# Two blocks of a transformer on one core: another order of the first loads and products, and the gather for the first experts

## The chip, the cores and the metric

The kernel runs on one core of a Trainium2 chip. The metric is the device time of one execution in microseconds (us); three runs of the kernel before gave 2827.01 to 2830.11 us, median 2827.8.

## The reference, cut to what matters

Everything is float32, 256 tokens of width 1024. A first block of two layers (attention of two kinds and an MLP) is followed by a second block (a token mixer and a mixture of 16 experts).

```python
cos, sin = rope_tables(positions)
cond = jax.nn.silu(c)
for l in range(2):
    mod = (cond @ ada_w[l] + ada_b[l])                      # 1024 -> 6 * 1024
    shift_m, scale_m, gate_m, shift_f, scale_f, gate_f = jnp.split(mod, 6, axis=-1)
    h = rms_norm(x, norm_mix_g[l]) * (1.0 + scale_m) + shift_m
    proj = h @ w_in[l]                                      # queries, keys: norm, then rope
    ...
# second block, at its end:
gates, idx = lax.top_k(jnp.swapaxes(affinity, 1, 2), 32)    # each of 16 experts picks 32 of 256 tokens
xe = h[idx]
hid = silu(xe @ exp_w1) * (xe @ exp_w3)                     # 1024 -> 2048
ye = hid @ exp_w2 * gates                                   # 2048 -> 1024, added back at idx
```

## The kernel before, in words

**Loads.** SyncE walks through a list of weight chunks of 2 MB (`weight_chunks`) and loads each into a slot of SBUF as soon as the chunk that held the slot was used. For the first block there are four slots (the ring), for the experts six, and three more that are used once for the chunks of expert 0. What "used" means is a count of TensorE's jobs: SyncE waits on `bank_full` for the last job of the earlier chunk. The engines' orders are written out by hand; every engine works strictly in its own order. The class `Jobs` holds the order of all PSUM jobs; job n goes to bank n mod 8 and waits until job n - 8 was emptied by VectorE ("v") or ScalarE ("s").

**Head.** SyncE issues the vectors (0.22 MB: biases, gains, c) and then the ring: four chunks of ada_w for layer 0 in the order `ADA_ORDER = [2, 3, 0, 1]` (2 and 3 give scale, 0 and 1 give shift), then w_in. GpSimd issues, on its own queue, positions, lambdas, the early constants (identity, means), x, and, once the fourth chunk of ada_w has landed (L2167), the late constants. TensorE waits for vectors and `cond`, then per chunk makes a raw product (L2694, `four_sums`: 8 products of 512 columns in four strips), which ScalarE copies out, and later turns the sum into columns with four small products (L2686); VectorE adds the bias. Before the third chunk TensorE waits for constants and x and transposes x (L2698, 16 transposes, four banks, copied to `xT` by VectorE, L2494). Before the fourth it takes the mean of squares of x (L2717), for which ScalarE squares `xT` (L2205). VectorE starts with the angles of rope and the lambdas (L2465 to L2487), ScalarE with the sines (L2249 to L2253) right after the silu. At the end VectorE scales `xT` into `hT` (`scaled`, L2395), ScalarE adds the shift slice by slice (`shifted`, L2222), and TensorE starts on the columns of queries and keys (L2686), two `columns` of 256 tokens per job, whose squares ScalarE takes (L2285). GpSimd rotates them (L2181) with `rope`.

**Experts.** The one-hot matrix `E_SEL` (tokens by 16 x 32 places) picks each expert's tokens. For expert 0 a product with its 32 columns gives `xc` (jobs "xc"); the gather for all 16 experts (jobs "xe", eight times two products of 512 columns) runs inside expert 0, four j after the second quarter of its first layer and four after the third. From then on VectorE copies the next expert's columns of it to `E_XC`. An expert uses 12 chunks: w1 and w3 by quarters (L2694), small turnings (L2686), then w2 by quarters and `combine`. Expert 0 is written out, experts 1 to 14 are a loop, expert 15 is written out.

Of the kernel before, what the change touches and what calls it, by code (L numbers as in the profile page):

```python
# [9 lines left out]
ALU = mybir.AluOpType  # L10
# [408 lines left out]
class Jobs:  # L419


    def __init__(self):
# [3 lines left out]
        for n, c in enumerate(ADA_ORDER):  # L426
            if n == 2:
                for tt in range(TT):
                    for q in range(2):
                        add(("xT", tt, q), "v")  # L430
            if n == 3:
                add(("norm", "mix", 0), "s")
            self.modulations([("ada", 0, c)])
# [105 lines left out]
    def second_block(self):  # L539
# [74 lines left out]
        for e in range(N_EXP):  # L614
            for q in range(4):
# [24 lines left out]
GATHERED_AFTER = [(), (0, 1, 2, 3), (4, 5, 6, 7), ()]  # L640
# [14 lines left out]

EXPERT_JOBS = 24
# [20 lines left out]
E_XE, E_EARLY, E_XTOK, E_GAIN, E_H2, E_ACC = 0, 4096, 4096, 6144, 9472, 9472  # L677
E_U, E_SQ, E_DIAG = 7424, 0, 2048
# [3 lines left out]
def build(nc, t, out):  # L682
# [24 lines left out]
    with ExitStack() as ctx:  # L707
# [297 lines left out]
        def second_pool(pool, chain):  # L1005
# [55 lines left out]
            pool.wait_ge(xc_ready, N_EXP - 1)  # L1061
# [3 lines left out]
        def second_scalar(act, chain, free, norm, shifted):  # L1065
# [149 lines left out]
            def expert(k0, more, done):  # L1215
                for q in range(4):
# [43 lines left out]
            expert(0, 0, free)  # L1260
            with act.Fori(1, N_EXP - 1) as e:
                expert(1, e - 1, free.looped)
            free.skip(N_EXP - 2)
# [8 lines left out]
        def second_vector(dve, chain, free, norm):  # L1272
# [332 lines left out]
            for tt in range(TT):  # L1605
                last = one_hot(tt, 0, 1)
            last.then_inc(chosen, 1)
            for tt in range(TT):
                last = one_hot(tt, 1, N_EXP)
# [3 lines left out]
            def expert(k0, e, more, done):  # L1613
# [12 lines left out]
                if k0 == 0:  # L1626
                    emptied(dve, ("xe", KT - 1))
                if k0 < N_EXP - 1:
# [28 lines left out]
            expert(0, 0, 0, free)  # L1657
            with dve.Fori(1, N_EXP - 1) as e:
                expert(1, e, e - 1, free.looped)
            free.skip(N_EXP - 2)  # L1660
# [14 lines left out]
        def second_tensor(pe, start, finish, chunk, product, four_sums, turn, columns, norm, normed, done):  # L1675
# [44 lines left out]

            def keep_busy(b, n):

                for _ in range(n):
                    nc.tensor.matmul(b[:, :], ident, cst[:, 0:512], start=True, stop=True)  # L1724
# [305 lines left out]
            emptied(pe, ("slotT", 0))  # L2030

            def expert(k0, e, more):
# [31 lines left out]
                xc, hid = ar(E_XC, KT, CAP), ar(E_HID, 16, CAP)  # L2064
                if k0 == 0:
                    emptied(pe, ("xc", 0, 1))
                else:
                    pe.wait_ge(xc_ready, e)
                for q in range(4):
# [19 lines left out]
                    if k0 == 0:  # L2089
# [18 lines left out]
            expert(0, 0, 0)  # L2108
            with pe.Fori(1, N_EXP - 1) as e:
                expert(1, e, e - 1)  # L2110
            done[0] += EXPERT_JOBS * (N_EXP - 2)
# [6 lines left out]
        def _(sp):  # L2118
            def middle_experts():
                first = chunk_at[("w1", 2, 0)]  # L2120
                with sp.Fori(2, N_EXP - 1) as e:
                    for i in range(12):
                        n = first + i
                        key, name = chunks[n][0], chunks[n][1]
                        sp.wait_ge(bank_full, jobs.last_job_of_chunk[chunks[n - EXPERT_SLOTS][0]] + 1 + (e - 2) * EXPERT_JOBS)
# [4 lines left out]
            sp.dma_start(vec[:, :], t["vectors"]).then_inc(vectors_loaded, 16)  # L2130
            for n, (key, *_rest) in enumerate(chunks):
                if key[0] in ("w1", "w2", "w3") and 2 <= key[1] < N_EXP - 1:
                    if key == ("w1", 2, 0):
# [62 lines left out]
        def _(act):  # L2196
# [51 lines left out]
            act.wait_ge(angles_ready, 1)  # L2248
            nc.scalar.activation(rope[:, 1, :], ar(0, SEQ), ACT.Sin, scale=col("rot_sign")).then_inc(rope_ready, 1)  # L2249
            act.wait_ge(angles_ready, 2)  # L2250
            nc.scalar.activation(rope[:, 0, :], ar(256, SEQ), ACT.Sin).then_inc(rope_ready, 1)
            act.wait_ge(lam_sums, 1)
            nc.scalar.activation(lamv[:, 0:2 * DEPTH], lamv[:, 4:4 + 2 * DEPTH], ACT.Exp).then_inc(lam_exp, 1)  # L2253
            for n, c in enumerate(ADA_ORDER):
                if n == 3:
                    emptied(act, ("xT", 1, 1))
                    norm("mix", 0, xT, None, None)
                modulations([("ada", 0, c)])
            modulations([])

            for l in range(DEPTH):
# [106 lines left out]
        def _(dve):  # L2368
# [95 lines left out]
            dve.wait_ge(small_loaded, 32)  # L2464
# [608 lines left out]
```

## Time and profile before

| | us |
|---|---|
| three runs, median | 2827.8 |
| profiled execution | 2835.8 |
| its span | 2833.9 |
| TensorE busy | 2527.0 (89%) |
| VectorE busy | 894.4 (32%) |
| ScalarE busy | 532.3 (19%) |
| granted TensorE clock, mean | 0.925 |

The span runs from the first to the last instruction that the profile shows. TensorE's matmuls are pipelined, so its busy time holds waits inside a matmul as well. Each product of float32 stands as two records. The granted clock is 1.00 or 0.50 of 2.4 GHz; a value between them is a mixture in the window. 666.85 MB are moved; an expert chunk is 2048 KB, 192 of them are the experts'.

### The profile page before, as it was taken

To read this page: it belongs to the slowest core of one execution; us is meant where nothing else is said; L and a number is where in the kernel's file an instruction comes from. 1 tells how busy PE (TensorE), PEld (TensorE's weight loads), DVE (VectorE), ACT (ScalarE), POOL (GpSimd) and SP (SyncE) were. 2 spreads that over 40 slices of the span, in tenths; PEclk is the share of its full clock that TensorE was granted. 3 is DMA by queue.
4 is the path that set the end of the run, shared out by engine and by line. 5 is a ranking of instruction groups with operands and counts; after the bars stand their busy time and mean duration, and the time that the engine had idled before them with its cause. 6 is when DMAs were issued, how large, how long until landed. Compare 5 with 4: busy or idle time off the path is not lost.

```text
span 2833.9 us, 36842 instructions
## 1 busy us (share of the span) xinstructions
PE 2527.0 (89%) x15512; PEld 1792.9 (63%) x15512; DVE 894.4 (32%) x1609; ACT 532.3 (19%) x1063; POOL 154.2 (5%) x146
## 2 busy tenths in 40 slices
PE   5999989999999899999989999999877777777777
PEld 4857678887867788887568888864433333333333
DVE  2743524202735412313575641231111111111112
ACT  2115411001126212002234432121000000000001
POOL 0320000000310000000011110100000000000000
PEclk8999999999999999999999999989788887878888
DMA  7335447545332463453000002548999999999998
GB/s 298 137 139 231 195 184 278 221 150 210 146 134 75 149 256 132 182 234 115 1 1 1 1 2 97 214 196 366 428 428 429 428 428 429 429 428 428 429 429 356
DMA packets 48787, 666.85 MB, mean 235 GB/s; under 512 B 5531, under 2 KB 5702, under 8 KB 7585
## 3 DMA queue, kind: packets, MB, share of 16 engines
q1 hardware_dynamic: 46656, 656.65, 57.0%
q0 software_dynamic: 2016, 8.53, 0.9%
q8 instruction: 90, 1.47, 0.2%
q14 instruction: 25, 0.20, 0.0%
HBM read 664.11 MB, written 1.05 MB: 235 GB/s over the span
## 4 chain that ended last, share of the span: by engine, by line
PE 64%; DMA 26%; DVE 6%; ACT 2%; issue 1%; POOL 0%; DVEq 0%; ACTq 0%; POOLq 0%
PE bank L2686 51%; DMA ring<-exp_w 24%; PE bank L2694 6%; PE bank L2698 2%; PE bank L2910 2%; DVE arena L2420 1%; PE bank L1886 1%; DMA arena<-x 1%; DMA arena<-exp_w 1%; PE bank L2717 1%; PE bank L1914 1%; PE bank L1724 1%; ACT hT L2222 0%; DVE hT L2563 0%; ACT arena L2346 0%
## 5 line engine op out<-in xcount | busy, mean ns | idle before, releaser
L2686 PE MATMUL bank<-hT,ring 128*128 128x256 f32 (+2 forms) x3232 | 740.3, 389 | 11.3 <-ACT hT L2222 11.3
L2686 PEld LDWEIGHTS bank<-hT,ring 128*128 128x128 f32 x3232 | 607.7, 192 | 146.3 <-issue 70.9
L2694 PE MATMUL bank<-ring,arena 128*32 128x512 f32 (+1 forms) x2496 | 322.8, 659 | 170.2 <-DMA ring<-exp_w 157.2
L2686 PE MATMUL bank<-arena,ring 128*128 128x256 f32 x1600 | 352.1, 381 | 6.7 <-POOL arena L2189 2.8
L2686 PEld LDWEIGHTS bank<-arena,ring 128*128 128x128 f32 x1600 | 304.2, 191 | 50.0 <-POOL arena L2189 3.6
L2694 PEld LDWEIGHTS bank<-ring,arena 128*32 128x32 f32 x2496 | 88.2, 130 | 357.0 <-issue 209.7
L2686 PEld LDWEIGHTS bank<-vec,arena 128*128 128x128 f32 x1344 | 177.6, 213 | 74.6 <-issue 67.6
L2686 PE MATMUL bank<-arena 64*128 64x128 f32 (+4 forms) x1156 | 207.7, 378 | 4.7 <-ACT arena L2329 1.6
L2694 PE MATMUL bank<-arena 128*32 128x256 f32 (+1 forms) x1568 | 162.4, 557 | 39.8 <-DMA arena<-exp_w 39.4
L1623 DVE COPY arena<-bank 128x512 f32<-128x512 f32 x64 | 44.3, 692 | 481.7 <-PE bank L2694 481.7
L2686 PE MATMUL bank<-vec,arena 128*128 128x32 f32 (+2 forms) x1344 | 183.1, 289 | 3.9 <-DVE arena L2420 3.4
L2686 PEld LDWEIGHTS bank<-arena 64*128 64x128 f32 (+1 forms) x1156 | 139.1, 196 | 66.3 <-issue 48.7
L2694 PEld LDWEIGHTS bank<-arena 128*32 128x32 f32 x1568 | 57.2, 128 | 128.8 <-issue 64.6
L2529 DVE RECIPROCAL arena<-arena 128x512 f32<-128x512 f32 x28 | 93.9, 3353 | 84.3 <-ACT arena L2274 84.3
L2686 PE MATMUL bank<-ring 128*128 128x128 f32 (+1 forms) x1024 | 110.2, 268 | 5.1 <-DVE ring L1442 4.9
L2686 PEld LDWEIGHTS bank<-ring 128*128 128x128 f32 (+1 forms) x1024 | 107.0, 183 | 8.0 <-DVE ring L1442 5.4
L2686 PE MATMUL bank<-ring,hT 128*128 128x512 f32 (+1 forms) x256 | 96.9, 539 | 0.0
L1218 ACT ACTIVATE arena<-bank 128x512 f32<-128x512 f32 x64 | 38.2, 597 | 288.9 <-PE bank L2694 288.9
L2686 PEld LDWEIGHTS bank<-ring,hT 128*128 128x128 f32 x256 | 48.6, 190 | 48.4 <-issue 46.9
L1645 DVE TENSOR_TENSOR arena<-arena,bank 128x256 f32<-128x256 f32 (+1 forms) x90 | 45.9, 510 | 99.5 <-PE bank L2686 99.1
L1250 ACT ACTIVATE arena<-bank 128x128 f32<-128x128 f32 x64 | 17.8, 278 | 312.3 <-PE bank L2686 312.3
L2644 DVE TENSOR_TENSOR arena<-arena,bank 128x512 f32<-128x512 f32 x32 | 22.0, 688 | 169.3 <-ACT arena L2356 169.3
(320 smaller groups left out, 2050.1 us busy)
## 6 DMA issues: line engine op xcount, KB each, us to landing
ring<-exp_w SPq DMA_DIRECT2D x125, 2048.0 KB, 26.2
arena<-exp_w SPq DMA_DIRECT2D x66, 2048.0 KB, 25.9
ring<-w_in SPq DMA_DIRECT2D x38, 2048.0 KB, 8.2
ring<-ada_w SPq DMA_DIRECT2D x24, 2048.0 KB, 7.9
ring<-w_mlp_up SPq DMA_DIRECT2D x16, 2048.0 KB, 7.8
ring<-w_mlp_down SPq DMA_DIRECT2D x16, 2048.0 KB, 7.7
ring<-mod_w SPq DMA_DIRECT2D x12, 2048.0 KB, 7.8
ring<-w_out SPq DMA_DIRECT2D x6, 2048.0 KB, 8.3
```

The source lines that it names most:

```text
L1218: done(sc.activation(raw_row(2 * q), b[:, :], ACT.Identity), ("up1", k0, q))
L1623: done(v.tensor_copy(raw_row(2 * q + 1), b[:, :]), ("up3", k0, q))
L1645: done(v.tensor_copy(acc, new) if k0 == 0 else v.tensor_tensor(acc, acc, new, ALU.add), key)
L1724: nc.tensor.matmul(b[:, :], ident, cst[:, 0:512], start=True, stop=True)
L1886: mms.append(nc.tensor.matmul(banks[par][:, p * 64:(p + 1) * 64], a, c, start=(i == 0), stop=(i == 1)))
L1914: mms.append(nc.tensor.matmul(banks[par][part, p * P:(p + 1) * P], a, c, start=(i == 0), stop=(i == 2)))
L2420: ins = v.scalar_tensor_tensor(out=row, in0=w[:, k], scalar=of(k), in1=row, op0=ALU.mult, op1=ALU.add)
L2529: chain(v.reciprocal(rs, rs))
L2686: mm = nc.tensor.matmul(out_, a, b, start=(i == 0), stop=(i == len(pairs) - 1))
L2694: mm = nc.tensor.matmul(o, a, b, start=(i < 4), stop=(i >= len(pairs) - 4))
L2698: return nc.tensor.transpose(out_, in_, ident[0:in_.shape[0], 0:in_.shape[0]])
L2910: mm = nc.tensor.matmul(banks[i][:, 0:SEQ], w[:, k, i * P:(i + 1) * P], ar(A_OA, 8, SEQ)[:, k], start=(k == 0), stop=(k == KT - 1))
```

## The change

Head: SyncE issues the early constants and x ahead of the ring; the vectors go to GpSimd's queue, first. GpSimd issues positions, lambdas and late constants only when the first chunk of w_in has landed. The transposes of x and the mean of squares stand ahead of all modulations on every engine. The angles, sines and lambdas are a function that VectorE and ScalarE call behind the scaled and shifted h. VectorE scales `xT` once the scale's chunks are there and takes the last two biases after it. TensorE gets unused products (`keep_busy`, each the identity by 512 columns of constants into the bank of the job to come): 2 and 3 ahead of the third and the fourth chunk's raw product, 4 ahead of the first query columns.

Experts: the first gather (jobs "xc") is for experts 0 and 1, 64 columns wide, copied to `E_XC` and `E_XC1`. The gather for all experts runs in expert 1 (2, 3 and 3 of the j after its second, third and fourth quarter). Expert 1 is written out, the loop is over experts 2 to 14. `E_ACC` and `E_U` change places, since the tokens in `E_H2` are now read until expert 1's end.

```diff
@@ Jobs
+        for tt in range(TT):
+            for q in range(2):
+                add(("xT", tt, q), "v")
+        add(("norm", "mix", 0), "s")
+        for c in ADA_ORDER:
             self.modulations([("ada", 0, c)])
@@
-                if e == 0:
+                if e == 1:
                     for j in GATHERED_AFTER[q]:
                         add(("xe", j), "s")
-GATHERED_AFTER = [(), (0, 1, 2, 3), (4, 5, 6, 7), ()]
+GATHERED_AFTER = [(), (0, 1), (2, 3, 4), (5, 6, 7)]
+FIRST_LOOPED = 2
-E_XE, E_EARLY, E_XTOK, E_GAIN, E_H2, E_ACC = 0, 4096, 4096, 6144, 9472, 9472
-E_U, E_SQ, E_DIAG = 7424, 0, 2048
+E_XE, E_EARLY, E_XTOK, E_GAIN, E_H2, E_ACC = 0, 4096, 4096, 6144, 9472, 7424
+E_U, E_SQ, E_DIAG, E_XC1 = 9472, 0, 2048, 11520
@@ ScalarE, experts
-                copy(key, ar(E_XC, KT, CAP)[:, 4 * half:4 * half + 4], P, CAP)
+                b = filled(act, key)[:, 0:2 * P].rearrange("p (a b) -> p a b", b=2 * CAP)
+                sc.activation(ar(E_XC, KT, CAP)[:, 4 * half:4 * half + 4], b[:, :, 0:CAP], ACT.Identity)
+                free(sc.activation(ar(E_XC1, KT, CAP)[:, 4 * half:4 * half + 4], b[:, :, CAP:2 * CAP], ACT.Identity), key)
@@ TensorE, experts
-                    mm = product(b[:, CAP * j:CAP * (j + 1)], [(ar(E_H2, TT, D)[:, tt, k * P:(k + 1) * P], ar(E_SEL + 512 * tt, CAP))
-                                                               for tt in range(TT)])
+                    mm = product(b[:, 2 * CAP * j:2 * CAP * (j + 1)],
+                                 [(ar(E_H2, TT, D)[:, tt, k * P:(k + 1) * P], ar(E_SEL + 512 * tt, 2 * CAP)) for tt in range(TT)])
-                if k0 == 0:
+                if k0 < 2:
                     emptied(pe, ("xc", 0, 1))
                 else:
-                    pe.wait_ge(xc_ready, e)
+                    pe.wait_ge(xc_ready, e - 1)
+                if k0 == 1:
+                    emptied(pe, ("slotT", 0))
@@ SyncE and GpSimd
-            sp.dma_start(vec[:, :], t["vectors"]).then_inc(vectors_loaded, 16)
+            sp.dma_start(cst[:, 0:C_LATE], t["consts"][:, 0:C_LATE]).then_inc(const_loaded, 16)
+            sp.dma_start(ar(A_WORK, TT, D), t["x"].rearrange("(a p) d -> p a d", p=P)).then_inc(x_loaded, 16)
@@
+            pool.dma_start(vec[:, :], t["vectors"]).then_inc(vectors_loaded, 16)
+            pool.wait_ge(slot_loaded[slot_of(FIRST_ADA)], 16 * loads(FIRST_ADA))
             pool.dma_start(posi, t["positions"].partition_broadcast(P)).then_inc(small_loaded, 16)
             pool.dma_start(lam, t["lambdas"]).then_inc(small_loaded, 16)
-            pool.dma_start(cst[:, 0:C_LATE], t["consts"][:, 0:C_LATE]).then_inc(const_loaded, 16)
-            pool.dma_start(ar(A_WORK, TT, D), t["x"].rearrange("(a p) d -> p a d", p=P)).then_inc(x_loaded, 16)
-            pool.wait_ge(slot_loaded[FIRST_ADA - 1], 16)
             pool.dma_start(cst[:, C_LATE:], t["consts"][:, C_LATE:]).then_inc(late_loaded, 16)
@@ VectorE, head
             dve.wait_ge(vectors_loaded, 16)
+            for tt in range(TT):
+                for q in range(2):
+                    b = filled(dve, ("xT", tt, q))
+                    free(v.tensor_copy(xT[...], b[...]), ("xT", tt, q))
+            rs = norm("mix", 0, None, None, None)
+            for c in ADA_ORDER[:-1]:
                 modulations([("ada", 0, c)])
...
                     scaled(xT, amp_mix, rs, hT[:, 0])
+                    modulations([("ada", 0, ADA_ORDER[-1])])
                     modulations([])
+                    rope_and_lambdas()
@@ TensorE, head
+            def keep_busy(b, n):
+                for _ in range(n):
+                    nc.tensor.matmul(b[:, :], ident, cst[:, 0:512], start=True, stop=True)
+            pe.wait_ge(const_loaded, 16)
+            pe.wait_ge(x_loaded, 16)
+            ...
+            norm("mix", 0)
             pe.wait_ge(vectors_loaded, 16)
             pe.wait_ge(cond_ready, 3)
+            for n, c in enumerate(ADA_ORDER):
+                modulations([("ada", 0, c)], (0, 0, 2, 3)[n])
             modulations([])
@@
+                        if (l, i) == (0, 0):
+                            keep_busy(start(("qk", 0, 0)), 4)
```

## Rows read from the trace of the kernel before

**Rows 1.** The page: DMA share by slices (section 2) and the chain by line (section 4).
```profile
DMA  7335447545332463453000002548999999999998
PE bank L2686 51%; DMA ring<-exp_w 24%; PE bank L2694 6%; PE bank L2698 2%; PE bank L2910 2%; DVE arena L2420 1%; PE bank L1886 1%; DMA arena<-x 1%; DMA arena<-exp_w 1%; PE bank L2717 1%; PE bank L1914 1%; PE bank L1724 1%; ACT hT L2222 0%; DVE hT L2563 0%; ACT arena L2346 0%
```

**Rows 2.** Chain of waits from 0 to 100 us: start, duration, what.
```profile
3.05 26.27 DMA arena<-x
...
29.46 3.65 PE bank L2698 x16
...
47.78 3.31 ACT hT L2222 x8
...
51.22 48.99 PE bank L2686 x207
```

**Rows 3.** Timeline from 0 to 75 us: start, duration, engine, line, operation.
```profile
11.03 3.47 PE L2694 MATMUL bank<-ring,hT 128*32 128x512 f32 x16 [11.03 <-DMA ring<-ada_w]
...
13.79 0.29 DVE L2465 CAST arena<-arena 128x256 f32<-128x256 int32 x1 [13.79 <-DMA arena<-lambdas]
...
20.24 0.20 ACT L2253 ACTIVATE lamv<-lamv 128x4 f32<-128x4 f32 x1 [0.21 <-DVE lamv L2479]
...
29.82 0.56 POOL L2168 DMA_DIRECT2D cst<-consts  x1 [26.06 <-DMA ring<-ada_w]
30.59 0.69 DVE L2494 COPY xT<-bank 128x512 f32<-128x512 f32 x1 [8.28 <-PE bank L2698]
...
36.32 1.99 ACT L2205 ACTIVATE arena<-xT 128x1024 f32<-128x1024 f32 x2
...
37.51 3.69 PE L2717 MATMUL bank<-arena,cst 128*128 128x256 f32 x16 [0.78 <-ACT arena L2205]
...
41.13 1.92 PE L2694 MATMUL bank<-ring,hT 128*32 128x512 f32 x16
...
42.99 1.95 PE L2686 MATMUL bank<-vec,arena 128*128 128x1 f32 x16
...
51.22 15.99 PE L2686 MATMUL bank<-hT,ring 128*128 128x256 f32 x64 [6.29 <-ACT hT L2222]
...
67.91 7.07 PE L2686 MATMUL bank<-hT,ring 128*128 128x256 f32 x32
```

**Rows 4.** DMA issues from 0 to 80 us: count, KB, us to landing.
```profile
arena<-lambdas POOLq DMA_DIRECT2D x1, 256.0 KB, 11.7
vec<-vectors SPq DMA_DIRECT2D x1, 216.5 KB, 2.5
arena<-positions POOLq DMA_DIRECT2D x1, 128.0 KB, 9.3
```

**Rows 5.** Stages of the head: busy by engine, then PEclk, DMA share, GB/s.
```profile
34.00:35.00 1.00, 1.00 (x12) 0.21 (x8) 0.00 (x0) 0.00 (x0) 0.00 (x0) 0.66 1.00 427
...
54.00:56.00 2.00, 2.00 (x8) 1.67 (x7) 0.00 (x0) 0.00 (x0) 0.00 (x0) 0.71 0.00 0
```

**Rows 6.** Timeline of TensorE from 1880 to 2080 us.
```profile
1898.92 7.03 PE L2686 MATMUL bank<-arena 128*128 128x32 f32 x32 [0.38 <-DVE arena L1603]
...
1918.21 7.03 PE L2686 MATMUL bank<-arena 128*128 128x512 f32 x16
```

**Rows 7.** Timeline of SyncE's loads from 1905 to 1960 us: start, time to the last.
```profile
1912.84 2.04 SPq L2149 DMA_DIRECT2D arena<-exp_w  x2
1916.28 23.63 SPq L2149 DMA_DIRECT2D ring<-exp_w  x4
1951.09 3.25 SPq L2149 DMA_DIRECT2D arena<-exp_w  x2
```

**Rows 8.** Stages of expert 0: busy of PE, PEld, DVE, ACT, POOL, then PEclk, DMA share, GB/s.
```profile
1930.00:1940.00 10.00, 10.00 (x47) 4.29 (x50) 0.29 (x1) 3.09 (x6) 0.00 (x0) 1.00 0.92 392
1940.00:1950.00 10.00, 9.24 (x95) 6.08 (x91) 1.90 (x5) 0.74 (x3) 0.00 (x0) 0.83 0.57 211
1950.00:1960.00 10.00, 10.00 (x112) 5.46 (x108) 3.93 (x9) 0.77 (x2) 0.00 (x0) 1.00 0.80 311
```

More of the change, by code:

```diff
@@ L1258, in second_scalar @@
                 key = ("xc", 0, half)
-                copy(key, ar(E_XC, KT, CAP)[:, 4 * half:4 * half + 4], P, CAP)
[L1260 to L1263, printed above, removed]
+                b = filled(act, key)[:, 0:2 * P].rearrange("p (a b) -> p a b", b=2 * CAP)
+                sc.activation(ar(E_XC, KT, CAP)[:, 4 * half:4 * half + 4], b[:, :, 0:CAP], ACT.Identity)
+                free(sc.activation(ar(E_XC1, KT, CAP)[:, 4 * half:4 * half + 4], b[:, :, CAP:2 * CAP], ACT.Identity), key)
+            for k0 in range(FIRST_LOOPED):
+                expert(k0, 0, free)
+            with act.Fori(FIRST_LOOPED, N_EXP - 1) as e:
+                expert(FIRST_LOOPED, e - FIRST_LOOPED, free.looped)
+            free.skip(N_EXP - 1 - FIRST_LOOPED)
             expert(N_EXP - 1, 0, free)
@@ L1605, in second_vector @@
             for tt in range(TT):
-                last = one_hot(tt, 0, 1)
+                last = one_hot(tt, 0, 2)
             last.then_inc(chosen, 1)
             for tt in range(TT):
-                last = one_hot(tt, 1, N_EXP)
+                last = one_hot(tt, 2, N_EXP)
             free(last, ("slotT", 0))
@@ L1655, in gate @@
                 done(v.tensor_tensor(ar(E_HID + 128 * q, 128), ar(E_SL + 128 * q, 128), b[:, 128:256], ALU.mult), key)
[L1657 to L1660, printed above, removed]
+            for k0 in range(FIRST_LOOPED):
+                expert(k0, k0, 0, free)
+            with dve.Fori(FIRST_LOOPED, N_EXP - 1) as e:
+                expert(FIRST_LOOPED, e, e - FIRST_LOOPED, free.looped)
+            free.skip(N_EXP - 1 - FIRST_LOOPED)
             expert(N_EXP - 1, N_EXP - 1, 0, free)
@@ L1672, in second_vector, with second_tensor @@
                                            op0=ALU.mult, op1=ALU.add).then_inc(x_final, 1)
-        def second_tensor(pe, start, finish, chunk, product, four_sums, turn, columns, norm, normed, done):
+        def second_tensor(pe, start, finish, chunk, product, four_sums, turn, columns, norm, normed, keep_busy, done):
             def spectrum(m):
@@ L2106, in expert @@
                     end(mm)
[L2108 to L2111, printed above, removed]
+            for k0 in range(FIRST_LOOPED):
+                expert(k0, k0, 0)
+            with pe.Fori(FIRST_LOOPED, N_EXP - 1) as e:
+                expert(FIRST_LOOPED, e, e - FIRST_LOOPED)
+            done[0] += EXPERT_JOBS * (N_EXP - 1 - FIRST_LOOPED)
             expert(N_EXP - 1, N_EXP - 1, 0)
@@ L2119, in middle_experts @@
             def middle_experts():
-                first = chunk_at[("w1", 2, 0)]
-                with sp.Fori(2, N_EXP - 1) as e:
+                first = chunk_at[("w1", FIRST_LOOPED + 1, 0)]
+                with sp.Fori(FIRST_LOOPED + 1, N_EXP - 1) as e:
                     for i in range(12):
@@ L2124, in middle_experts @@
                         key, name = chunks[n][0], chunks[n][1]
-                        sp.wait_ge(bank_full, jobs.last_job_of_chunk[chunks[n - EXPERT_SLOTS][0]] + 1 + (e - 2) * EXPERT_JOBS)
+                        sp.wait_ge(bank_full, jobs.last_job_of_chunk[chunks[n - EXPERT_SLOTS][0]] + 1 + (e - FIRST_LOOPED - 1) * EXPERT_JOBS)
                         _, _, _, _, rows, c0, w = chunks[n]
@@ L2471, in _ @@
-            chain(v.scalar_tensor_tensor(out=ar(256, SEQ), in0=ar(768, SEQ), scalar=-2 * PI, in1=ar(256, SEQ),
-                                         op0=ALU.mult, op1=ALU.add))
-            v.tensor_scalar(ar(256, SEQ), ar(256, SEQ), PI_IN, -PI_IN, ALU.min, ALU.max).then_inc(angles_ready, 1)
-            for l in range(DEPTH):
-                for i in range(2):
-                    a = lam[:, 256 * l + 128 * i:256 * l + 128 * i + 128]
-                    chain(v.tensor_tensor(ar(768, 64), a[:, 0:64], a[:, 64:128], ALU.mult))
-                    last = v.tensor_reduce(lamv[:, 4 + 2 * l + i:5 + 2 * l + i], ar(768, 64), AX.X, ALU.add)
-                    if (l, i) == (DEPTH - 1, 1):
-                        last.then_inc(lam_sums, 1)
-                    else:
-                        chain(last)
@@ L2723, in _, with modulations @@
             before = []
-            def modulations(now):
+            def modulations(now, unused=0):
                 for name, l, c in now:
+                    b = start((name + "_raw", l, c))
+                    keep_busy(b, unused)
                     w = chunk((name, l, c))
-                    b = start((name + "_raw", l, c))
                     finish(four_sums(b[:, :], [(cond(0 if name == "ada" else 1)[:, k], w[:, k]) for k in range(KT)]))
@@ L2980, in _ @@
                     mlp_columns(l, "down", j)
-            second_tensor(pe, start, finish, chunk, product, four_sums, turn, columns, norm, normed, done)
+            second_tensor(pe, start, finish, chunk, product, four_sums, turn, columns, norm, normed, keep_busy, done)
 H_BEFORE = [8 * i for i in range(len(NORMS))]
```

113 lines of the change are left out of this document (51 added, 62 removed).

## The prediction

> **What bounds the kernel now.** I read the page's slices first [rows 1]: the DMA digits are 0 in slices 20 to 24 and stand at 8 or 9 from slice 28 on, and the chain charges 24% of the span to transfers of expert weights. So there are two regimes: up to about 1900 us TensorE sets the time, from there the stream of 2 MB expert chunks. A saving in the head passes through the first regime as a shift, since SyncE's later loads wait for TensorE's own jobs; in the second, only a shift of the stream counts.
>
> The chain of waits for the head [rows 2] shows x under way from 3.05 to 29.33 us, transposes at 29.46, the last shift of h begun at 47.78 and the first query columns at 51.22. TensorE does little before 29 us. The head's timeline [rows 3] says what is in series after x.
>
> The stream: SyncE can load the tenth expert chunk only when the second is used, at 1912.84, and the sixteenth at 1951.09 [rows 7]. Between these the stage windows show 392, 211 and 311 GB/s [rows 8] instead of the 427 of a full window [rows 5]: (35 + 216 + 116) x 10 us = 3.7 MB, 8.6 us of an idle queue, with TensorE busy 10.00, 9.24 and 10.00 of each 10 us. It was doing the gather for the other experts: two blocks of four products, 7.03 us each [rows 6].
>
> **Part 1, expert 0 and 1.** The gather (14.1 us) goes from expert 0 to expert 1. Every chunk use behind the first block comes 7.0 us earlier, behind the second 14.1 us earlier: the sixteenth chunk can be asked for at 1937. The six chunks asked for from 1912.84 on take 6 x 2.1 MB / 0.43 = 29 us, to about 1944 with some 2 us to start. The last of the six can be asked for at 1939.6 - 14.1 = 1925.5 (its slot goes with the second block now [rows 7]). The queue no longer runs dry, and all behind it moves by what the gap was, 8.6 us; less if part of the restart remains, so I take 8.0.
>
> In expert 1 the same 14.1 us stand among uses that are paced by the stream, 12 x 4.9 = 59 us an expert. TensorE begins expert 1 at about 1945, some 10 us behind that chunk's landing (the fourth of the six, 1912.8 + 2 + 4 x 4.9 = 1934.5); six slots allow it to be some 22 us behind (five loads less the start of one) before the stream waits. Its own work there at full clock is twelve chunk uses of 1.92 and four turnings of 1.95 [rows 3] and eight combining products of 0.44, 34 to 40 us with the small waits; with the gather 54, under 59. Hidden; if the clock is low in there the cover is gone (a rival below).
>
> On the path to 1912.84 something is added: each of the 16 first gather products is 64 columns wide instead of 32. This width stands in no row at low clock. The 32 records of it took 7.03 us, 220 ns each [rows 6]. Lower end 0, since a record of 512 columns took only 439 ns at full clock [rows 6] and 64 columns at half clock would be about 110 ns, inside 220; upper end 32 x 32 columns x 1.7 ns = 1.8 us if it adds up. Nearest is the lower: 0.2. ScalarE copies twice per half, +0.3 us. Net of part 1: 8.0 - 0.5 = 7.5 us, ends 5 and 8.6. The one-hot for two experts, the moved accumulator, the moved slot wait and the static copy of expert 1 cost under 0.1 us: they are a few more elements, or only another address, or a wait for something done long before.
>
> **Part 2, the head.** SyncE now issues constants (0.3 MB) and x (1.05 MB) ahead of the ring. From 2 us at 0.43 MB a us that is 5.3 us, say x at 6. The vectors (0.22 MB) go to GpSimd's queue; VectorE waits for them before the transposed copies and ScalarE before everything. Lower end 3.3 us, where they land now; upper end 10.6, where the positions land, first of that queue now [rows 4]. Nearest is the positions' row, but the vectors' neighbours are smaller rows at first: I take 8.5.
> In the Trainium skill, "DMA: Bandwidth & Descriptors", section "Anatomy of one DMA", a GpSimd-issued transfer costs 2.0 us plus bytes over 436 GB/s; that would put the vectors at 3.8 us. The trace speaks against using it here: positions, half that size, took 9.3 us [rows 4] with the ring's loads beside them. By the page the sum would be 1.5 us better, no more, since the transposes then end last.
>
> Then, by durations of [rows 3]: transposes 6 to 9.7 at low clock (3.65, [rows 2]); four copies of 0.7 end at 11.5; squares from there, 1.0 each; the mean from 12.6. Its 16 records took 3.69 at full clock; the first half goes at low clock, and the clock in these rows rose 4 to 5 us after TensorE began (at 29.46, level 0.66 in 34 to 35; at 51.22, level 0.71 in 54 to 56 [rows 5]). Mean done at about 18.5.
>
> From there TensorE has, back to back, four raw products of 1.92, four turning products of 1.0 (1.95 for two), and 2 + 3 + 4 = 9 unused products of 0.88 (16 records in 7.03 [rows 6]): 7.7 + 4.1 + 7.9 = 19.7 us. Query columns start at 38.2. Which waits are beside it: the last modulation chunk now lands at 29.8 at most (GpSimd's wait for it ends there, [rows 3]); with positions and lambdas behind it (0.38 MB, 0.9 us) 28.9; it is wanted at 30.6. First w_in chunk 4.9 later, 33.8. VectorE's eight scalings (3.3 us) now run once chunk 3's bias is there, beside raw products; the last bias and the first shift take 0.7 us after TensorE's last turning product (34.7), beside the four unused products (3.5). So without these four the start would be at 35.4, and of the nine unused ones some 7 us are on the path. What they hold: the clock. Now the first 64 column records take 15.99 us, after that 32 take 7.07 [rows 3]: 1.9 us back. Head: 51.2 - 38.2 + 1.9 = 14.9.
>
> **Small loads.** Positions, lambdas and late constants wait for the first w_in chunk (32.4 to 33.8). GpSimd's three issues queue nothing else until the first rotation. Lambdas took 11.7 us from issue [rows 4], so they land at 44.8 to 46.2. VectorE and ScalarE both wait there in order: rope and lambdas took from 13.79 to 20.44 [rows 3], 6.7 us, so ScalarE is free for the first square of the query columns at 51.5 to 52.9, plus 0.6. TensorE asks for it two columns in, at 38.2 + 14.1 = 52.3. A stall of 0 to 1.2: I take 0.5. The same loads share the queue with w_in chunks that TensorE uses at 14 to 15 us each against 4.9 of loading: hidden. Head net 14.4. Lower end 8: vectors at 10.6 (2.1), the mean wholly at low clock (1.5), one raw and one unused product more so (2.4), the rest small waits. Upper end 17: vectors so early that the transposes end last (1.1), x a little earlier, no stall.
>
> **Sum.** 14.4 + 7.5 = 21.9 us. The profiled execution took 2835.8 (span 2833.9 and 1.9 around it), 8.0 above the median of the runs; it would be 2813.9, and the median 2827.8 - 21.9 = 2805.9.
>
> **Rivals.**
> (a) The wait for rope takes the place of the one removed. x took 26.3 us on GpSimd's queue beside the ring's loads [rows 2]. If the small loads, which now meet three queued w_in chunks, take that long, they land at 58.7, ScalarE has squared at 66.0, and TensorE stands from 52.3 for 13.7 us instead of 0.5: total gain 8.7, 2819.1. Against it: 9.3 and 11.7 us for just these two in the same company [rows 4].
> (b) The stream's gap stays: the queue runs dry in expert 1 instead. For: TensorE is late there already by 10 us. Against: the 59 us cadence with 54 of work. Gain 14.4 - 0.5, 2813.9.
> (c) Both (a) and (b): 21.9 - 13.2 - 8.0 = 0.7 of gain, 2827.1, no change.
> (d) Slower: the clock. One mechanism: TensorE stays at the lower level (0.50, 1.2 GHz) where both parts put work. A raw product there is 3.47 [rows 3], an unused one 1.76, 32 records of a small turning 7.03 [rows 6]. Head: mean until 20, then 4 x 3.47 + 4.1 to 8 + 15.8 = 34 to 38: columns at 55.8, 4.6 us later than now. Expert 1: twelve uses of 3.47, four turnings of 3.5 and 8 us of combining, 64 us, and 28 of gather, against 59 of cadence and 12 of slack (22 - 10): 21 us of idle queue in place of 8.6. Total 4.6 + 12.4 + 0.5 = 17.5 us slower, 2845. It decides from the point where the level in 20 to 38 us stays at 0.50. For: it took TensorE from 29.46 until 34 to 35 us to get off it [rows 5]. Against: in the new order TensorE has no gap from 12.6 on, and the stretch with the gather in expert 0, just as full, shows 1.00 in 1930 to 1940 [rows 8].
>
> **Numbers.** Forecast 0.70, (a) 0.12, (b) 0.10, (c) 0.04, (d) 0.04. Less than 0.2% (5.7 us) this kernel's measurement can't tell from none. Faster: 0.92, same 0.04, slower 0.04. The ends of the head (8, 17) and of the stream (5, 8.6) give 2802 to 2814.8; with 2 us of spread and (a), which lies at 2819.1, the range is 2799 to 2819.
>
> **What would show it.** Transposes at about 6 to 10 us and not after 10.6; vectors landed by 8.5; PEclk 1.00 from 18 to 38; query columns begun at 38 (right) or after 45 (wrong); 64 records of them in 14.1; a wait of TensorE over 2 us for the first square of the query columns speaks for (a). In the stream: full windows in each 10 us window from 1905 on (shifted time), no SyncE wait of 12 us behind TensorE in expert 0; end of the span 22 us earlier. If the windows in expert 1 are full and the span is shorter by under 15 us, my head is wrong; if the head is right and there is a dip, it is (b).

## The result, and the profile after

| | before | changed |
|---|---|---|
| median of 5 runs each | 2830.1 us (2827.0 to 2839.4) | 2801.3 us (2797.3 to 2812.6) |
| ratio, 95% interval | | 0.9898 [0.9870, 0.9927] |
| profiled execution, its span | 2835.8, 2833.9 | 2801.7, 2799.5 |

Faster by 1.0%: 28.8 us between these medians, where 21.9 were forecast. The changed kernel run a second time, against seventeen runs of the one before, gave 2804.4 us, ratio 0.9914 [0.9895, 0.9934], 24.5 us (by the interval 18.7 to 29.7). Single runs of one kernel lie up to 15 us apart (2797.3 to 2812.6 above; 2824.7 to 2839.3 among the seventeen), so the steps are judged by milestones of the traces. One run of lazy_no4 below was in a slow state (3956.5 us at a mean granted clock of 0.588) and is left out of its median.

The page of the changed kernel; its DMA line answers to [rows 1]:
```profile
DMA  8336547545331473453000002559999999999998
...
PE 63%; DMA 27%; DVE 7%; ACT 2%; issue 1%; POOL 0%; DVEq 0%; SPq 0%; ACTq 0%
```
Slices 27 and 28 have gone from 4 and 8 to 5 and 9: the stream has no dip any more. The two regimes are as before.

**Head.** Timeline of the changed kernel from 0 to 52 us (start, duration, engine, line, operation, idle time before and its releaser), answering to [rows 3]:
```profile
7.09 3.65 PE L2701 MATMUL bank<-cst,arena 128*128 128x128 f32 x16 [7.09 <-DMA arena<-x]
7.42 0.81 ACT L2246 ACTIVATE hT<-vec 128x256 f32<-128x256 f32 x3 [5.39 <-DMA vec<-vectors]
...
10.77 0.69 DVE L2469 COPY xT<-bank 128x512 f32<-128x512 f32 x1 [0.16 <-PE bank L2701]
...
12.60 3.72 PE L2725 MATMUL bank<-arena,cst 128*128 128x256 f32 x16 [1.87 <-ACT arena L2205]
...
31.81 3.68 PE L2706 MATMUL bank<-cst 128*128 128x512 f32 x8
...
32.19 3.30 ACT L2222 ACTIVATE hT<-hT,mod 128x256 f32<-128x256 f32 x8 [1.45 <-DVE mod L2408]
...
32.91 0.55 POOL L2166 DMA_DIRECT2D arena<-positions  x1 [30.90 <-DMA ring<-w_in]
...
35.63 14.05 PE L2689 MATMUL bank<-hT,ring 128*128 128x256 f32 x64
...
43.71 0.29 DVE L2477 CAST arena<-arena 128x256 f32<-128x256 int32 x1 [11.55 <-DMA arena<-lambdas]
...
50.16 0.20 ACT L2260 ACTIVATE lamv<-lamv 128x4 f32<-128x4 f32 x1 [0.21 <-DVE lamv L2491]
...
50.99 1.10 PE L2689 MATMUL bank<-arena,cst 128*128 128x512 f32 x2 [1.31 <-ACT arena L2287]
```
The milestone is the first mean of the query columns' squares, the last row. In the kernel before it is this row of TensorE's timeline:
```profile
67.05 1.02 PE L2686 MATMUL bank<-arena,cst 128*128 128x512 f32 x2
```
It began at 67.05 us before and begins at 50.99 now: 16.1 us. The columns themselves begin 15.6 us earlier, and their first 64 records take 14.05 for 15.99 [rows 3]; 1.31 us goes back in the stall ahead of the last row.

The chain of waits of the changed kernel over the same stretch (start, duration, what):
```profile
1.19 5.76 DMA arena<-x
...
18.24 14.37 DMA ring<-w_in
...
32.91 0.54 POOL arena L2166
33.45 10.23 DMA arena<-lambdas
...
50.16 0.20 ACT lamv L2260
```
x no longer leads: it is done at 6.95. From 18 us the chain runs through the first w_in chunk, which lets GpSimd ask for the small loads, then the lambdas, VectorE's rope and ScalarE's lambdas. TensorE's back-to-back work, the forecast's path, ends within 1.3 us of it. Both paths are nearly equally long, which matters for every experiment on this stretch.

DMA issues of the changed kernel from 0 to 80 us (count, KB, us to landing), answering to [rows 4]:
```profile
arena<-x SPq DMA_DIRECT2D x1, 1024.0 KB, 5.8
...
arena<-lambdas POOLq DMA_DIRECT2D x1, 256.0 KB, 10.2
vec<-vectors POOLq DMA_DIRECT2D x1, 216.5 KB, 6.1
arena<-positions POOLq DMA_DIRECT2D x1, 128.0 KB, 7.7
```

**Stream.** TensorE's timeline and SyncE's loads after the gather, answering to [rows 6] and [rows 7]:
```profile
1874.89 7.01 PE L2689 MATMUL bank<-arena 128*128 128x64 f32 x32 [0.44 <-DVE arena L1605]
```
```profile
1887.52 2.04 SPq L2150 DMA_DIRECT2D arena<-exp_w  x2
1890.95 9.80 SPq L2150 DMA_DIRECT2D ring<-exp_w  x4
1911.52 3.24 SPq L2150 DMA_DIRECT2D arena<-exp_w  x2
```
Restart (the load that waits for the second chunk's use) to end of span was 1912.84 to 2833.9, 921.1 us; it is 1887.52 to 2799.5, 912.0. So 9.1 us come from the stream. Four loads are asked for in 9.80 us where it took 23.63 [rows 7]. The gather for two experts takes 7.01 us, as the one 32 columns wide did (7.03 [rows 6]).

Stages of the changed kernel (busy of PE, PEld, DVE, ACT, POOL, then PEclk, DMA share, GB/s), answering to [rows 8]; the last two hold the moved gather in expert 1:
```profile
1930.00:1940.00 10.00, 9.34 (x58) 4.23 (x57) 0.95 (x3) 2.26 (x6) 0.00 (x0) 1.00 1.01 426
1940.00:1950.00 10.00, 10.00 (x60) 4.46 (x58) 0.96 (x2) 2.39 (x4) 0.00 (x0) 1.00 1.01 431
1950.00:1960.00 10.00, 9.24 (x71) 5.49 (x74) 0.90 (x4) 2.35 (x5) 0.00 (x0) 1.00 1.00 424
```
TensorE is as full as it was in expert 0, but the queue stays full beside it.

**The middle.** Head 16.1 and stream 9.1 make 25.2 of the 34.4 us between the two spans. The other 9.3 lie between the first mean and the restart: 1845.8 us before, 1836.5 now. ScalarE's events run parallel, 16 us apart, until 1720; by 1750 they are 22 apart. Another 1.7 come at about 1880, where 32 narrow products took 5.46 us before and 3.75 now, and most of the rest lies behind the start of the first gather. The kernel before at the first place (columns as above):
```profile
1715.00:1720.00 5.00, 5.00 (x35) 4.55 (x35) 0.00 (x0) 1.37 (x4) 0.00 (x0) 0.74 0.98 413
1720.00:1725.00 5.00, 4.22 (x23) 3.73 (x24) 0.00 (x0) 2.27 (x3) 0.00 (x0) 0.50 0.77 328
...
1740.00:1745.00 5.00, 5.00 (x23) 3.99 (x21) 0.00 (x0) 0.66 (x2) 0.00 (x0) 0.66 0.00 0
```
and the changed one, which passes the same work at full clock:
```profile
1715.00:1720.00 5.00, 5.00 (x37) 4.39 (x35) 0.00 (x0) 0.60 (x1) 0.00 (x0) 1.00 0.00 0
1720.00:1725.00 5.00, 5.00 (x27) 4.35 (x27) 0.00 (x0) 0.66 (x2) 0.00 (x0) 1.00 0.01 3
```
No instruction of this stretch was changed. What the experiments say of it stands below.

### The profile page after: what moved, and what is told of

Its sections match the earlier page's. It is cut to its first block, busy times and chain, and to the rows that moved or that the text cites. A ratio compares the mean times of both kernels' runs of the same rounds, so it can differ in the third digit from the quotient of the medians.

```text
span 2799.5 us, 36794 instructions
## 1 busy us (share of the span) xinstructions
PE 2506.8 (90%) x15530; PEld 1778.1 (64%) x15530; DVE 894.2 (32%) x1608; ACT 534.8 (19%) x1067; POOL 153.5 (5%) x145
## 4 chain that ended last, share of the span: by engine, by line
PE 63%; DMA 27%; DVE 7%; ACT 2%; issue 1%; POOL 0%; DVEq 0%; SPq 0%; ACTq 0%
PE bank L2689 50%; DMA ring<-exp_w 25%; PE bank L2697 6%; PE bank L2701 2%; PE bank L2919 2%; DVE arena L2422 1%; PE bank L1884 1%; DMA ring<-w_in 1%; DVE hT L2566 1%; PE bank L2725 1%; PE bank L1912 1%; DMA arena<-exp_w 1%; ACT arena L2348 0%; PE bank L2939 0%; DVE ring L1441 0%
## 5 line engine op out<-in xcount | busy, mean ns | idle before, releaser
L2697 PE MATMUL bank<-arena 128*32 128x256 f32 (+1 forms) x1568 | 156.7, 541 | 42.0 <-DMA arena<-exp_w 41.5
L1217 ACT ACTIVATE arena<-bank 128x512 f32<-128x512 f32 x64 | 38.2, 597 | 288.2 <-PE bank L2697 288.2
```

What stands on the lines that cost most here:

```text
L1217: done(sc.activation(raw_row(2 * q), b[:, :], ACT.Identity), ("up1", k0, q))
L2697: mm = nc.tensor.matmul(o, a, b, start=(i < 4), stop=(i >= len(pairs) - 4))
```

## The experiments

Each kernel is compared with the kernel before on the same chip, in three groups: down to after_again (median of the kernel before 2828.9 us, 17 runs), down to small_late (2829.9, 7 runs), and the rest (2830.3, 10 runs). Two milestones recur: the **first mean** of the query columns' squares, and **restart to end**. The column before the last gives the start of the query columns and the first mean.

| kernel | runs | median, us | ratio [95%] | columns, first mean | restart to end |
|---|---|---|---|---|---|
| head_only | 6 | 2807.3 | 0.9928 [0.9909, 0.9947] | 38.60, 52.48 | 920.6 |
| experts_only | 12 | 2824.0 | 0.9984 [0.9973, 0.9996] | 50.04, 65.46 | 912.1 |
| after_again | 6 | 2804.4 | 0.9914 [0.9895, 0.9934] | 37.36, 51.25 | 913.3 |
| no4 | 3 | 2807.7 | 0.9906 [0.9874, 0.9937] | 37.55, 53.41 | 912.1 |
| no9 | 3 | 2810.9 | 0.9919 [0.9875, 0.9963] | 34.34, 50.87 | 913.5 |
| small_early | 3 | 2802.1 | 0.9904 [0.9853, 0.9955] | 37.72, 51.60 | 911.9 |
| small_late | 3 | 2807.6 | 0.9916 [0.9884, 0.9949] | 35.74, 55.75 | 911.7 |
| extra_e0 | 5 | 2813.3 | 0.9945 [0.9926, 0.9963] | 35.73, 51.02 | 920.9 |
| extra_e1 | 2 | 2802.1 | 0.9895 [0.9870, 0.9921] | 37.19, 51.08 | 913.9 |
| lazy_no4 | 3 | 2798.0 | 0.9894 [0.9867, 0.9922] | 34.44, 51.10 | 912.0 |
| best | 4 | 2790.9 | 0.9859 [0.9841, 0.9876] | 34.72, 48.60 | 913.6 |

By the ratios only experts_only and best stand clear of after_again; the intervals of the others overlap its own. What is said of them rests on one trace each.

**The two parts alone, and the whole again.** head_only takes the edits of the head and the small loads, experts_only those of experts 0 and 1.

> The head's part of the change alone; the experts are as before. In the changed kernel's trace the first mean of the query columns' squares stands at 50.99 us against 67.05 before, and from there to 1720 us the two traces run parallel. Theory (the two parts add, the rest is the clock's spread): 16 us faster than before, first mean at 51, and the idle stretch of the stream in expert 0 back. Rival (the head shifts later stages onto a better clock, a lasting effect): about 16 + 7 = 23 us faster, with the level at 1.00 from 1700 to 1730 in the trace.

> The experts' part alone; the head is as before. Theory: the idle queue of 8.6 us in expert 0 goes, from the stream's restart (SyncE's load after the second chunk) to the end 912 us instead of 921; 9 us faster. Rival: part of the gap comes back in expert 1, where the gather is now; under 6 us faster and a 10 us window under 400 GB/s there.

> The changed kernel again, beside its two parts. If the parts add: 25 us faster than before (16 + 9); what lies above that in the recorded pair (28.8 in the medians, 34.4 in the two traces) is spread of the clock between 1715 and 1745 us. If a lasting effect of both parts together: 29 or more again.

The traces separate cleanly. head_only keeps the old restart to end (920.6) and its dip; its stages, columns as above:
```profile
1910.00:1920.00 10.00, 9.24 (x84) 5.50 (x80) 1.47 (x4) 1.18 (x4) 0.00 (x0) 0.82 0.65 244
1920.00:1930.00 10.00, 10.00 (x117) 5.17 (x110) 2.23 (x4) 0.49 (x2) 0.00 (x0) 0.83 0.52 185
```
experts_only keeps the old head (first mean 65.46) and has the short stream (912.1). By medians the parts give 21.6 and 4.8 us, 26.4 together, against 24.5 to 28.8 for the whole: additive within the scatter. How the sum divides is less clear. The 4.8 of experts_only are less than the 9.0 by which its restart to end is shorter, and its interval reaches only to 7.6. The 21.6 of head_only are more than its first mean shows (52.48 us against 65.46 and 67.05 with the old head, 13.0 to 14.6), its interval begins at 15.0, and its trace has level 1.00 from 1700 to 1730. That is what the rival named for this run, a lasting effect of the head on the clock of later stages. It is not excluded; point 8 below returns to it.

**Is it TensorE's load in expert 0 that stops the stream?** Sixteen unused products, 14 us, go into the changed kernel, in expert 0 (extra_e0) or, on top of the gather that is there, in expert 1 (extra_e1):
```
+                    if k0 == 0 and q in (1, 2):      # extra_e1: k0 == 1
+                        keep_busy(begin(("up1", k0, q + 1)), 8)
```

> The changed kernel with 16 unused products of 512 columns (14.1 us of TensorE) in expert 0, eight after each of the two middle quarters, where the gather stood before. Theory (the gap of the stream is TensorE's time in expert 0, while only six slots come free): from the stream's restart to the end 912 us become about 921, and a window of 10 us in expert 0 falls under 300 GB/s. Rival (the gain has another source, the static expert 1 or the moved buffers): stays at 912.

> The same 16 unused products in expert 1, on top of the gather. Theory (expert 1 has slack: TensorE waits for chunks there and may fall 22 us behind): restart to end stays at 912, windows stay full. Rival (expert 1 was at its limit): it grows by 5 us or more.

extra_e0 brings back the long stream exactly, 920.9. Its loads and stages:
```profile
1883.74 23.62 SPq L2152 DMA_DIRECT2D ring<-exp_w  x4
```
```profile
1900.00:1910.00 10.00, 10.00 (x57) 4.22 (x55) 0.69 (x1) 0.60 (x1) 0.00 (x0) 1.00 0.85 324
1910.00:1920.00 10.00, 9.24 (x88) 5.60 (x88) 1.00 (x3) 0.78 (x3) 0.00 (x0) 0.66 0.38 161
```
The 23.62 us for four loads are the 23.63 of [rows 7], with other instructions in the gather's place. It is TensorE's time that counts, not what it computes. In extra_e1 28 extra us lie in one expert and only one window dips:
```profile
1970.00:1980.00 10.00, 9.24 (x120) 5.94 (x119) 1.99 (x5) 1.26 (x3) 0.00 (x0) 1.00 0.88 338
```
(428 - 338) x 10 us is 0.9 MB, 2.1 us of queue; restart to end is 913.9, 1.9 above the changed kernel's (the kernels without added work lie at 911.7 to 913.6). Expert 1 has room for the 14 us of gather and nearly for as much again.

**The unused products ahead of the columns.** no4 leaves out the four at the end of the modulations, no9 also the five between them.
```
-                        if (l, i) == (0, 0):
-                            keep_busy(start(("qk", 0, 0)), 4)
 # no9 also: (0, 0, 2, 3)[n] -> (0, 0, 0, 0)[n]
```

> The changed kernel without the four unused products ahead of the query columns. The prediction on record had them on the path with 3.5 us. Theory from the new trace: the path runs over the first w_in chunk, the small loads and rope to ScalarE's first square (50.3 us), so the columns begin near 32.8 instead of 35.63 and the first mean of their squares stays at 51, gain 0. Rival (they are on the path): first mean at 48. Second rival (they hold the clock): the columns' 64 records take 16 us instead of 14.05.

> The changed kernel without any of the nine unused products. TensorE then waits for each ada_w chunk: gaps of some 2 to 3 us. Theory: last raw product begins at the landing (26.6), 1.5 us earlier; columns near 32.8, first mean at 51, no gain. Rival (the clock falls in the gaps): raw products of 3.4 us instead of 1.92 and 64 column records of 16 us, first mean still at 51 or up to 52.

Both were expected to begin the columns near 32.8. They began at 37.55 and 34.34; TensorE's timeline of no4 and of no9:
```profile
37.55 16.02 PE L2689 MATMUL bank<-hT,ring 128*128 128x256 f32 x64 [3.68 <-ACT hT L2222]
```
```profile
34.34 16.43 PE L2689 MATMUL bank<-hT,ring 128*128 128x256 f32 x64 [3.68 <-ACT hT L2222]
```
Where 3.68 us of unused products were, TensorE stands idle for 3.68 us, waiting for ScalarE's shifts. The columns wait for the last of the eight shifts, not for the first: the program builds the list of (weights, slice of h) pairs before it issues the first product, and each slice's wait is issued while the list is built. The four cost nothing: the columns of after_again, whose mean of squares of x took 5.41 us as that of no4 did, began at 37.36, those of no4 at 37.55. And they hold the clock: in all seven traces with the four the first 64 records take 14.05 us. Stages of no4, the idle stretch, the first columns and what follows:
```profile
33.90:37.50 3.60, 0.00 (x0) 0.00 (x0) 0.16 (x1) 3.37 (x9) 0.78 (x2) 0.61 0.99 386
37.60:41.60 4.00, 4.00 (x10) 3.20 (x11) 0.00 (x0) 1.11 (x1) 0.00 (x0) 0.51 0.96 323
41.60:43.60 2.00, 2.00 (x11) 1.77 (x10) 0.00 (x0) 0.00 (x0) 0.00 (x0) 1.00 1.08 458
```
After TensorE has stood still the level is at 0.51 (the lower, 1.2 GHz) for the first 4 us of columns; in the changed kernel it is 1.00 from 34 to 40. The 64 records take 16.02 us instead of 14.05, and the first mean comes 2.2 us later than in after_again. In no9 the columns begin 3.2 us earlier than in no4, although the mean of squares of x took 6.65 us there instead of 5.41. Without that difference it would be 4.4, the length of five unused products: the five are on the path. TensorE did not stand between the raw products, where gaps of 2 to 3 us were expected. With 16.43 us for the 64 records the first mean is at 50.87, level with the changed kernel (50.99 and 51.25).

**When the small loads start.** Positions and lambdas wait for the first w_in chunk; small_early makes them wait for the second ada_w chunk (the late constants stay where they were), small_late for the second w_in chunk (the late constants too).
```
-            pool.wait_ge(slot_loaded[slot_of(FIRST_ADA)], 16 * loads(FIRST_ADA))
+            pool.wait_ge(slot_loaded[slot_of(1)], 16 * loads(1))
 # small_late: FIRST_ADA + 1 in both places
```

> Positions and lambdas are issued when the second ada_w chunk has landed (about 16.5 us) instead of the first w_in chunk; late constants as in the changed kernel. Theory (small loads and rope are on the path): they land near 27, rope is done at 37 to 38, ScalarE squares when the first columns end; TensorE's stall of 1.3 us before the first mean goes: mean at 49.7 plus at most 1 for the ring's delay. Rival (the ring's delay costs more): the first w_in chunk lands 2 us or more later than 32.6 and the columns begin behind 37.

> Positions, lambdas and late constants wait for the second w_in chunk (about 5 us later). If the small loads are on the path: the first mean moves from 51 to 55 or 56, and nothing else does. If TensorE's own products set the time: it stays under 52.

small_late, VectorE's and TensorE's timeline:
```profile
48.47 0.29 DVE L2477 CAST arena<-arena 128x256 f32<-128x256 int32 x1 [16.20 <-DMA arena<-lambdas]
```
```profile
55.75 2.05 PE L2689 MATMUL bank<-arena,cst 128*128 128x512 f32 x2 [5.95 <-ACT arena L2287]
```
The loads go out 4.9 us later (37.84) and the first mean is 4.8 us later: one for one, the wait of rival (a) in miniature. small_early has no stall, but its ring is late (timeline of it, GpSimd and TensorE):
```profile
16.94 0.55 POOL L2166 DMA_DIRECT2D arena<-positions  x1 [14.93 <-DMA ring<-ada_w]
...
35.21 0.54 POOL L2169 DMA_DIRECT2D cst<-consts  x1 [17.19 <-DMA ring<-w_in]
```
```profile
30.24 1.92 PE L2698 MATMUL bank<-ring,hT 128*32 128x512 f32 x16 [0.52 <-DMA ring<-ada_w]
```
The fourth ada_w chunk lands at 30.2 us instead of 26.5 and GpSimd's wait for the first w_in chunk ends at 35.2 instead of 32.9. I had expected at most 1 us, by their bytes (0.38 MB). The first mean is at 51.60, where after_again, with the same 5.41 us for the mean of x, has 51.25: the earlier start gains nothing, and a start between the two was tried in the last kernel.

**The wait spread over the products.** lazy_no4 is no4 with each slice's wait issued ahead of its own product:
```
-                    mm = product(b[:, i * SEQ:(i + 1) * SEQ],
-                                 [(w[:, k, j * P:(j + 1) * P], rhs(k)) for k in range(count)])
+                    for k in range(count):
+                        mm = nc.tensor.matmul(b[:, i * SEQ:(i + 1) * SEQ], w[:, k, j * P:(j + 1) * P], rhs(k), ...
```

> The changed kernel without the four unused products, and with TensorE's waits for the slices of h placed between the products instead of all ahead of the first one (in the list of pairs all eight are issued before a product is). In the kernels so far the columns began 0.1 us after the last of the eight shifts (35.49 to 35.60 in the changed one, 51.08 to 51.22 before). Theory: columns begin 0.1 us after the first shift or with the first w_in chunk, near 33 instead of 37.55 without the four, and the clock holds; the first mean stays at 51, since rope's wait holds ScalarE; the other four norms may give up to 3 us each. Rival (the wait isn't the reason): columns again at 37 or later.

Timeline of lazy_no4, ScalarE and TensorE:
```profile
33.79 3.30 ACT L2222 ACTIVATE hT<-hT,mod 128x256 f32<-128x256 f32 x8 [1.45 <-DVE mod L2408]
34.44 15.69 PE L2713 MATMUL bank<-hT,ring 128*128 128x256 f32 x64 [0.89 <-ACT hT L2222]
```
TensorE now idles 0.89 us and starts 0.65 behind the first shift: the cause named for no4 holds. The clock did not hold, as I had expected it to: the 64 records take 15.69 us, and from 34 to 38 us the level is 0.57. In best below, behind the same 0.89 us of idle time, they take 14.05. What decides between the two is open. The first mean stays at 51.10, with a stall of 0.97 for ScalarE's square. So the small loads' path is a second limit, as the chain said.

**best** is lazy_no4 (the waits spread, the four left out) with two things more: positions and lambdas after the fourth ada_w chunk, and eleven instead of nine unused products ahead of the slots' transposes.
```
 # lazy_no4, and in the small loads: slot_of(3), loads(3)
-            keep_busy(b, 9)
+            keep_busy(b, 11)
```

> As the kernel with waits between products, and with positions and lambdas issued when the fourth ada_w chunk has landed (26.5) instead of the first w_in chunk, and eleven instead of nine unused products ahead of the slots' transposes. Theory: small loads land near 37, rope is done at 44, columns begin with the first w_in chunk, which two small loads delay to 34 or 35, first mean at 49 instead of 51. The two more unused products fill TensorE's 1.7 us wait before the slots; if the clock then holds through the first gather, that takes 4 us instead of 7. Altogether 3 to 8 us faster than the changed kernel. Rival: the w_in chunk comes so late that nothing is won, and the clock falls all the same: same as the changed kernel.

Timelines of best, the head and TensorE ahead of expert 0:
```profile
34.72 14.05 PE L2714 MATMUL bank<-hT,ring 128*128 128x256 f32 x64 [0.89 <-ACT hT L2223]
48.60 1.02 PE L2690 MATMUL bank<-arena,cst 128*128 128x512 f32 x2
```
```profile
1855.99 9.71 PE L2707 MATMUL bank<-cst 128*128 128x512 f32 x22
...
1866.56 3.79 PE L2690 MATMUL bank<-arena 128*128 128x64 f32 x32 [0.44 <-DVE arena L1605]
```
2790.9 us in the median: 39.5 under the kernel before, and 10.5 to 13.5 under the changed one (its medians 2801.3 and 2804.4), more than the 3 to 8 expected. Against lazy_no4 on the same chip it is 7.2. In the traces the first mean is 2.4 us earlier than in the changed kernel, the gather's start 8.3 and the restart 12.9. In the changed kernel TensorE has 18 records of unused products there and then 1.72 us of idle time for VectorE, and the gather goes at level 0.50 (1875 to 1881); here it has 22 and no such gap, and the gather goes at 1.00. The gather's pace gives 3.2 us (3.79 for 7.01) and the products behind it 1.4 (5.36 for 6.73). That the two added products did it is not shown. The changed kernel's second trace has the old 18 records, 1.90 us of idle time behind them, and the short gather (TensorE's timeline):
```profile
1881.60 3.79 PE L2689 MATMUL bank<-arena 128*128 128x64 f32 x32 [0.44 <-DVE arena L1605]
```
Of the ten traces with 18 such records and the 64-wide gather, five take 3.79 to 4.61 us and five 7.00 to 7.09. The five short ones are those with a dip of the clock some 150 us earlier (point 8 below); best is the one trace with a short gather and no such dip, which speaks for the two products but is a single trace. The 5.9 us between first mean and gather were not separated either: the waits are spread in the other norms too, and the middle scatters by itself.

## Why the prediction was right, and what in it was not

1. **The order of the head: right.** Transposes at 7.09 to 10.74 (said: 6 to 10), vectors by 8.5 (7.4 at the latest), PEclk 1.00 from 18 to 38, 64 records in 14.05 (14.1), first w_in chunk at 32.6 (32.4 to 33.8). The columns started between 35.63 and 38.60 in the five traces with this head unaltered; 38.2 was said. One agreement is luck: the copies of x end at 11.46 (11.5 said) because two misses cancel. x landed at 6.95 and not at 6, and the vectors, said to hold the copies until 8.5, held nothing, since the last copy waits for the transposes. The prediction also prices earlier vectors at 1.5 us in one place and at 1.1 in another; only 1.1 follows from its own terms (copies done at 11.5 or at 10.4).

2. **The mean of squares of x, over-sized in one trace and not in others.** I gave it 5.9 us. It took 3.72 in the changed kernel's trace, its records at full pace at once, and 6.71 in head_only, with the same order and the same 1.87 us of idle before it:
```profile
12.58 6.71 PE L2718 MATMUL bank<-arena,cst 128*128 128x256 f32 x16 [1.87 <-ACT arena L2198]
```
This explains 2.2 of the 2.6 us by which the columns came early, and all of the 3.0 us between the earliest and the latest of those starts. The forecast could have given the term as a range; no single value was to be had.

3. **The failed step: "the last bias and the first shift take 0.7 us", "of the nine unused ones some 7 us are on the path".** The columns wait for all eight shifts, 3.3 us. Four of the nine (3.68 us) lie beside that wait and cost nothing; no4, no9 and lazy_no4 show it. The start time came out right all the same, by luck: the four fill just the time that the shifts take. A wrong answer was given only to a question that the change does not ask: what the columns would do without the four. The trace of before had the answer, had I looked: the last shift ends at 47.78 + 3.31 = 51.09 [rows 2] and the columns start at 51.22.

4. **The rope wait: right in kind, small in size.** Lambdas land at 43.7 (said: 44.8 to 46.2), the stall is 1.31 us (0.5; ends 0 and 1.2), larger because the columns were earlier. In after_again, head_only and extra_e1, whose columns began at 37.19 or later, there was no stall. Rival (a) needed 13.7. Its mechanism is real, one for one in small_late, but the loads took 10.2 us from issue and not 26.

5. **Head term.** 16.1 us in the recorded pair against 14.4. By other traces: 65.46 for the old head (experts_only), 51.25 and 52.48 for the new one, so 13.0 to 16.1. The term was right; 14.4 lies near the middle of what it varies over.

6. **Stream term.** 9.0 us net against 7.5. Restart to end holds only the closing of the gap: 9.1, where I took 8.0 of 8.6. What was to be paid ahead of the restart came to 0.1 instead of 0.5: the 64-wide gather cost nothing (0.2 said), and ScalarE's double copies put 0.12 us more on the wait (0.53 for 0.41), where 0.3 was said. Nine traces with the new order and no added work lie at 911.7 to 913.6, extra_e1 at 913.9; the three with 14 us more in expert 0 at 920.6 to 921.1. So 7.0 to 9.4. Rivals (b) and (c) are out: no window of 10 us of the changed kernel from 1890 to 2780 us is below 424 GB/s.

7. **Rival (d)**: the level in 20 to 38 us did not stay at 0.50, and stood at 1.00 beside the moved gather. Out at both of its places.

8. **What no step spoke of: 9.3 us of the middle.** The stretch from first mean to restart took 1845.8 us before, 1836.5 after, 1838.4 in after_again, 1832.1 in head_only, and 1836.1 in experts_only, which has the old head. no9 took 1846.6, best 1826.0. A dip of the clock somewhere from 1700 to 1745 us shows in before, experts_only, after_again, no9, small_early and extra_e1, and is absent in the others. The same kernel shows both; the changed kernel's second trace has it (level 0.50):
```profile
1700.00:1710.00 10.00, 9.22 (x55) 7.62 (x56) 0.00 (x0) 3.73 (x6) 0.00 (x0) 0.50 0.63 270
```
So the 9.3 us of the recorded pair need not be the change's. That the change has no part in them is not shown: both traces with the old head have the dip and only four of the eleven with the new one, and head_only gained more by medians than by its first mean. Two traces with the old head are too few to settle it. What decides whether the clock falls there stays open. The two parts are worth 20.0 to 25.5 us by their milestones (13.0 + 7.0 to 16.1 + 9.4), the second comparison gave 24.5, and 21.9 was said; the rest of the 28.8 between the first medians is scatter or such an effect.

## What to carry to other kernels

Before pricing a filler or a wait, see what the instruction behind it really waits for: compare the end of the releasing group with the start of the released one, for the first and for the last of its members. Unused products are free only beside such a wait. Here, beside 3.68 us of it, they paid by the clock; beside 0.89 us one trace kept the clock without them and one did not. Where a stage is bound by a stream whose slots the same engine frees, the engine's own work in the early stage decides, so move it to where the engine waits for the stream anyway. And when one execution's scatter is as large as the effect, compare milestones that enclose the change, not spans.

## What the runs showed of the hardware, not expected

- The same 16 records of the mean of squares of x took 3.72 to 6.71 us in executions of the same order, behind the same idle time. The granted clock does not tell the two apart: from 12.6 to 16 us it reads 1.00 in both, with 16 records in that window in the one and 8 in the other. So near to the start of work the pace of the records has to be read beside it.
- 0.38 MB in small loads on GpSimd's queue, set beside the ring's loads, delayed the ring's chunks by 2.3 to 3.7 us when asked for at 17 us (small_early), against 0.9 us by its bytes at 0.43 MB a us. Asked for at 26.8 us (best), it delayed the first w_in chunk by 0.5 us (GpSimd goes on at 33.37 for 32.91).
- 32 records of the gather took 7.01 us with 64 columns as with 32 (7.03) at the low clock, and 3.79 at level 1.00, where 32 records of 32 columns took 3.76. The time of so narrow a product goes with the clock and not with its width.
